# First layer's attention: the second head's q and k copied by VectorE, turned weights copied ahead of exponentials, weight roundings behind them

## What is computed

```python
def mla_mixer(c_q, c_kv, k_r, pos, q_norm, kv_norm, w_q_up, w_kv_up):
    q = (rms_norm(c_q, q_norm) @ w_q_up).reshape(B, S, MLA_HEADS, MLA_QK)
    q_nope, q_rope = q[..., :MLA_NOPE], rope(q[..., MLA_NOPE:], pos)
    kv = (rms_norm(c_kv, kv_norm) @ w_kv_up).reshape(B, S, MLA_HEADS, MLA_NOPE + MLA_V)
    k_nope, v = kv[..., :MLA_NOPE], kv[..., MLA_NOPE:]
    k_rope = jnp.broadcast_to(rope(k_r, pos)[:, :, None, :], (B, S, MLA_HEADS, MLA_ROPE))
    qf = jnp.concatenate([q_nope, q_rope], axis=-1)
    kf = jnp.concatenate([k_nope, k_rope], axis=-1)
    out = causal_block_attention(qf, kf, v, MLA_QK ** -0.5)
...
def memory_attention(q, k, v):
    s = jnp.einsum('bshd,bmhd->bhsm', q, k, preferred_element_type=jnp.float32) * (MEM_DIM ** -0.5)
    p = jax.nn.softmax(s, axis=-1)
    return jnp.einsum('bhsm,bmhd->bshd', p.astype(v.dtype), v)
```

## Time and profile before

| what | us |
|---|---|
| median of 3 runs | 1186.57 (1186.21 to 1186.69) |
| the profiled execution, device time | 1186.46 |
| its span (first to last instruction) | 1184.7 |
| TensorE busy | 1163.5 (98%) |
| ScalarE busy | 604.0 (51%) |
| VectorE busy | 540.8 (46%) |
| GpSimd busy | 459.8 (39%) |

### The profile page before, as it was taken

One profiled execution on the slowest core, in us unless ns is written; L12 is line 12 of the kernel. 1 busy time (PEld: TensorE's weight loads), 2 busy tenths in 40 slices (PEclk: granted clock), 3 DMA queues, 4 the chain that ended last, 5 costly groups with the idle time before them and its releaser, 6 DMA issues.

```text
span 1184.7 us, 16023 instructions
## 1 busy us (share of the span) xinstructions
PE 1163.5 (98%) x5967; PEld 913.9 (77%) x5967; DVE 540.8 (46%) x987; ACT 604.0 (51%) x1266; POOL 459.8 (39%) x331
## 2 busy tenths in 40 slices
PE   8999999899999999999999999999999999999998
PEld 7988866578988666668888987787666677888886
DVE  4311575645110655454466546612787860033333
ACT  7344677755352655564545654534655553243242
POOL 6534721134344222314343322445444443444461
PEclk9999999999999999999999999999999999999999
DMA  8443211113335322212331322233222113232321
GB/s 301 144 107 69 65 23 48 54 58 88 96 100 137 96 72 71 72 37 74 107 89 54 117 61 65 78 89 107 62 63 54 54 54 89 90 107 89 106 89 71
DMA packets 111573, 100.99 MB, mean 85 GB/s; under 512 B 21168, under 2 KB 98300, under 8 KB 111496
## 3 DMA queue, kind: packets, MB, share of 16 engines
q1 hardware_dynamic: 108952, 95.38, 27.6%
q0 software_dynamic: 864, 3.15, 0.7%
q10 hardware_dynamic: 1680, 1.44, 0.4%
HBM read 97.83 MB, written 2.12 MB: 84 GB/s over the span
## 4 chain that ended last, share of the span: by engine, by line
PE 91%; DVE 3%; ACT 3%; issue 2%; DMA 1%; POOL 1%; SPq 0%; DVEq 0%; ACTq 0%
PE bank L607 49%; PE bank L2054 8%; PE bank L1712 7%; PE bank L1504 6%; PE bank L912 3%; PE bank L878 3%; PE bank L896 2%; PE bank L2070 2%; PE bank L2082 2%; PE bank L2094 2%; PE bank L1296 1%; PE bank L1801 1%; DMA w_raw<-in_w_mem_kv 1%; POOL w_lo L526 1%; PE bank L717 1%
## 5 line engine op out<-in xcount | busy, mean ns | idle before, releaser
L526 POOL TENSOR_TENSOR w_lo<-w_raw,w_hi 128x1024 fp32r<-128x1024 f32 (+4 forms) x157 | 352.9, 2249 | 632.6 <-ACT w_hi L511 632.6
L511 ACT ACTIVATE w_hi<-w_raw 128x1024 fp32r<-128x1024 f32 (+6 forms) x161 | 159.2, 989 | 228.7 <-PE bank L607 200.2
L607 PE MATMUL bank<-acts_hi,w_hi 128*128 128x512 f32 (+1 forms) x576 | 224.2, 389 | 0.9 <-POOL w_lo L526 0.9
L607 PE MATMUL bank<-acts_lo,w_hi 128*128 128x512 f32 (+1 forms) x576 | 222.7, 387 | 0.0
L607 PE MATMUL bank<-acts_hi,w_lo 128*128 128x512 f32 (+1 forms) x576 | 222.6, 386 | 0.0
L607 PEld LDWEIGHTS bank<-acts_hi,w_hi 128*128 128x128 f32 x576 | 108.2, 188 | 24.4 <-POOL w_lo L526 1.5
L607 PEld LDWEIGHTS bank<-acts_lo,w_hi 128*128 128x128 f32 x576 | 108.2, 188 | 21.9
L607 PEld LDWEIGHTS bank<-acts_hi,w_lo 128*128 128x128 f32 x576 | 108.3, 188 | 21.3
L2189 DVE TENSOR_TENSOR_SCAN arena_end<-arena,junk 128x512 f32<-128x512 f32 (+3 forms) x64 | 72.8, 1138 | 58.3 <-ACT arena L2139 58.3
L607 PE MATMUL bank<-w_hi,acts_hi 128*128 128x512 f32 (+4 forms) x240 | 87.0, 362 | 0.4 <-POOL w_lo L526 0.3
L607 PE MATMUL bank<-w_hi,acts_lo 128*128 128x512 f32 (+4 forms) x240 | 86.2, 359 | 0.0
(11 more groups left out here) (307 smaller groups left out, 2153.5 us busy)
## 6 DMA issues: line engine op xcount, KB each, us to landing
w_raw<-in_w_in SPq DMA_DIRECT2D x64, 512.0 KB, 3.7
w_raw<-in_w_out SPq DMA_DIRECT2D x24, 512.0 KB, 3.6
w_raw<-in_w_in_b SPq DMA_DIRECT2D x22, 512.0 KB, 3.8
w_raw<-in_w_in_a SPq DMA_DIRECT2D x10, 512.0 KB, 4.2
w_raw<-in_w_mem_kv SPq DMA_DIRECT2D x8, 512.0 KB, 8.3
w_raw<-in_w_sb_proj SPq DMA_DIRECT2D x8, 512.0 KB, 3.4
w_raw<-in_w_ssd_proj SPq DMA_DIRECT2D x8, 512.0 KB, 3.4
arena_shared<-f_kept_rows SPq DMA_DIRECT2D x11, 256.0 KB, 4.4
```

Of the source, the lines that this page charges most:

```text
L511: nc.scalar.activation(w_at(p)[0][:, 0:size], w_raw[p % RAW][:, 0:size], ACT.Copy).then_inc(w_high.sem, 1)
L526: nc.gpsimd.tensor_tensor(lo[:, 0:size], w_raw[p % RAW][:, 0:size], hi[:, 0:size].bitcast(F32), ALU.subtract).then_inc(w_rest.sem, 1)
L607: mm = nc.tensor.matmul(bank_of(S, s, g)[0:lhs.shape[1], 0:rhs.shape[1]], lhs, rhs, start=j + kk + t == 0, stop=j == len(S.pieces) - 1 and ...
```

## The change

Three things change in steps 8 to 27 of the first layer's sweep; the number of instructions stays the same in total but for the copies' engine.

1. `collect` copies only the first head's half on ScalarE, for all products but the first two (`BY_BOTH`). The second head's half is a new VectorE instruction in `collect_second` (a multiplication by the same scale), which stands in `early` of the even steps, ahead of the maxima of the next step. It counts `qk_second`. The next product waits for both counts, and so do the first scores of a pair.
2. In the odd steps 9 to 27 the copies of turned weights run ahead of the exponentials (`copies_first`).
3. The weight rounding leaves `after` of the even step and stands in `between` of the odd step that follows, behind its exponentials.

```diff
-        def sweep_act(act, A, between, after, lag=1):
+        def sweep_act(act, A, between, after, lag=1, copies_first=()):
...
-            copies_first = (steps - 4, steps - 3, steps - 1)
+            copies_first = (*copies_first, steps - 4, steps - 3, steps - 1)
...
+        qk_second = count("qk_second")
+        BY_BOTH = 2
...
         def mla_pair(p):
+            second_in = ((qk_second.sem, 2 * p + 2 - BY_BOTH),) if p else ()
...
-                        ((qk_made.sem, 2 * p + 2), rope_in, pA_v.evac(2 * MB)))
+                        ((qk_made.sem, 2 * p + 2), rope_in, pA_v.evac(2 * MB)) + second_in)
...
                     if q:
                         pe.wait_ge(qk_made.sem, q)
+                    if q > BY_BOTH:
+                        pe.wait_ge(qk_second.sem, q - BY_BOTH)
...
+        def head_of_step(s):
+            return 2 * (s // 4 - MP) + 2 + s % 4 // 2
...
-                for e in range(2):
+                for e in range(2 if q < BY_BOTH else 1):
                     rows = slice(e * HD, (e + 1) * HD)
                     ins = nc.scalar.activation((aqT2, akT2)[q % 2][e][p % 2][rows], bank[0][rows, :], ACT.Copy,
...
                 if 4 * MP <= s < last and s % 2 == 0:
-                    q = 2 * (s // 4 - MP) + 2 + s % 4 // 2
-                    collect(q)
-                    split_ahead_act(act, S, 0, q)
+                    collect(head_of_step(s))
...
+            def between(s):
+                if 4 * MP < s <= last and s % 2:
+                    split_ahead_act(act, S, 0, head_of_step(s - 1))
...
-            sweep_act(act, attA, lambda s: None, after, lag=2)
+            sweep_act(act, attA, between, after, lag=2, copies_first=range(4 * MP + 1, last, 2))
...
+            def collect_second(q):
+
+                p, rows = q // 2, slice(HD, 2 * HD)
+                dve.wait_ge(C["product"].sem, pA_qk.done_after(0, q, 0))
+                if p >= 2:
+                    dve.wait_ge(*attA.scored(4 * (MP + p - 1)))
+                nc.vector.tensor_scalar((aqT2, akT2)[q % 2][1][p % 2][rows], bank[0][rows, :],
+                                        (QK_A ** -0.5, 1.0)[q % 2], None, ALU.mult).then_inc(qk_second.sem, 1)
...
+                if 4 * MP <= s < last and s % 2 == 0:
+                    collect_second(head_of_step(s))
```

## The result

| | before | after |
|---|---|---|
| median of 6 runs each, side by side, us | 1186.45 | 1177.3 (1176.98 to 1177.77) |
| the profiled execution, device time / span | 1186.46 / 1184.7 | 1177.3 / 1175.5 |

The ratio is 0.9924, with a 95% interval of 0.9913 to 0.9934.

What follows compares the result with a forecast made beforehand. TensorE, nearly full, was held by waits before the eight turns and the 512 scores. A limit of 8.06 less 0.5 gave 7.56, said as 7.5; from 1186.46 that made 1179.0 us, range 1177.8 to 1182.6.

Steps and rivals of the forecast that it cites:

- the VectorE-bound rival: Engines reading one bank take turns, so the q copy takes 0.60 us longer and VectorE becomes the bound; 1183.5 us, chance 0.14.
- 13.0 to 13.3: Forecast stretch in us between q products, in place of 14.71, with the first 0.4 less.
- That is a tie: From 256 maxima to second 512 scaling, VectorE needs 7.51 us and TensorE 7.61, so the q copy just fits.
- the 0.5 for it: Loss in us for the hand-over between engines, 0.1 in each pair, taken off the gain.
- VectorE's 7.51: VectorE's summed need in us from the 256 maxima to the second 512 scaling, new q copy included.
- at nothing: Cost given to the moved roundings, among other side effects, including the later GpSimd low parts.
- some 2 us later against TensorE: How much later a moved q rounding was said to end, relative to TensorE.
- the 1.40: TensorE's wait in us before the eight turns of a pair, blamed on ScalarE's late copies; all of it was to go.
- the tail ... 0.3 either way: Stretch behind the loop's end at 230.41 us, said to have the same instructions; allowed 0.3 us up or down.
- The low end of 1177.8: Fast end of the range in us: the limit of 8.06 with 0.3 from the tail and 0.3 for reading starts.
- the limit of 8.06: Most the loop of five pairs could gain in us: 69.13 less 61.07 of TensorE time without waits.
- The slower rival: GpSimd's low part for q holds the second 512 scaling, said to be clear by 1.39 us; 1191.7 us, chance 0.05.

Runs made afterwards that it cites:

- e6: The changed kernel with VectorE's copy of each second k half done twice, the extra one into scratch; 1180.06 us.
- e5: The changed kernel with VectorE's copy of each second q half done twice, the extra one into scratch; 1179.56 us.
- e3: The changed kernel with only the weight roundings put back in the even step, behind the half copy; 1180.70 us.
- e8: e3 with GpSimd made to wait, ahead of each low part, until VectorE has ended the running step's scalings; 1177.12 us.
- e12: The kernel before, with only a GpSimd wait ahead of each low part until VectorE has ended the running step's scalings; 1184.39 us.
- e2: The changed kernel with ScalarE's old order of copies, exponentials and roundings back, the second head's halves staying on VectorE; 1181.46 us.
- e7: The kernel before with one part of the change alone, copies of turned weights ahead of the exponentials in the odd steps; 1182.34 us.
- e1: The changed kernel with the second head's half copies back on ScalarE, the new order there kept; 1178.88 us.
- e9: The changed kernel with the last pair's gating product moved behind the scalings of the 256-column step; 1177.62 us.

## Why the prediction was wrong in size

**Right.** What bound the loop (the eight turns behind ScalarE's copies, the 512 scores behind the k copy), that both waits go, that TensorE is late next (busy for all of the 60.82), that the copies take 0.69, that the k copy lies inside VectorE's wait for the mask (though TensorE has only 0.06 to spare for it, e6), that a bank is read by two engines at once: the VectorE-bound rival needed turn-taking, and no row shows it. The Trainium skill (PSUM — Partial Sum Buffer, "PSUM bank collisions raise a hardware error") lets two engines read different quadrants of a bank together; the trace agrees, with 0.69 and 0.59 from the same 196.40. Pairs of 12.99 are just under the 13.0 to 13.3 that I named.

**Wrong: "That is a tie", and the 0.5 for it.** VectorE's 7.51 contained 2.96 "256 maxima, 384 scalings and the gating product". I took a stretch of the old timeline as the work in it. 0.64 of it was GpSimd holding two scalings (its low part of k the first, its copy the second), and the moved roundings take that away, so the stretch needs 7.51 - 0.64 = 6.87 against TensorE's 7.61. The copy of q must wait for the q product, so of the difference only some 0.16 can be used (e5); but that is room, not a loss. The hand-over cost nothing: 0.5 of the 1.65 by which I missed. Nor was it a tie with the hold left in: e3, which has it, takes 13.74 a pair, 0.76 more than after and not 0.1, and 0.59 of that lies where the 384 scalings and what follows them come late. I had weighed the same hold in the earlier trace rows, as a danger for the second 512 scaling, and not looked for it among the rows I was adding up.

**Wrong with it: the moved roundings "at nothing".** They cost nothing, and 3.4 us of the gain hang on them (e3), by GpSimd alone (e8). The "some 2 us later against TensorE" is wrong for q and was not asked for k: the low part of q starts 5.04 behind its q product, where it was 4.84, that of k 4.53 behind its k product, where it was 3.41. It is the 1.12 of the k part that ends the hold. I asked what a later low part would collide with, not what it would stop colliding with. With the hold gone the chain that starts at the 512 maxima starts earlier as well: e12 shows 0.53 a pair of the 1.40 that I put down to ScalarE's list going by that alone.

**Wrong: "the tail ... 0.3 either way".** It gave 0.72. ScalarE's timeline before, from the last collection on:

```profile
230.60 1.19 ACT L1357 ACTIVATE arena<-bank 64x512 f32<-64x512 f32 x2 [0.43 <-PE bank L1296]
231.82 1.06 ACT L511 ACTIVATE w_hi<-w_raw 128x1024 fp32r<-128x1024 f32 x1
...
235.55 0.69 ACT L952 ACTIVATE arena<-bank,stat 128x512 f32<-128x512 f32 x1
```

The same exponential after:

```profile
226.52 0.69 ACT L952 ACTIVATE arena<-bank,stat 128x512 f32<-128x512 f32 x1
```

Counted from the 256 scores of that pair (230.41 and 222.18), it starts at 5.14 and now at 4.34. Before, the two-half copy and a rounding of 1.06 stood ahead of what TensorE waits for. TensorE's next scores need the banks that these exponentials read; in its timeline before:

```profile
237.05 1.56 PE L878 MATMUL bank<-arena 128*128 128x384 f32 x4 [0.36 <-ACT arena L952]
```

Those scores start 6.64 behind the 256 scores before, and 6.02 after (228.20). "The same instructions" is true of the tail, but it begins with an edited collection and an edited order. The halves alone give all of it (e2: 13.63), the order alone two thirds (e7: 13.88; e1, with the moved roundings, 13.88 as well). This is the term that took the time below the range. The low end of 1177.8 left out the 0.5 and had 0.3 for the reading of starts, so the loop's 8.31 lies within it; the tail's 0.72 in place of 0.3 does not, nor does the 0.16 around the attention, for which I had no term and which stays unexplained (runs of after alone differ by up to 0.8).

**Mis-sized: the limit of 8.06.** The loop gave 8.31. The 512 scores with their mask were read as 1.93; unhindered they take 186.27 - 184.42 = 1.85. They take 1.91 to 1.94 in every run where they start behind a wait (before, e1, e6, e7, e12), so the old row had in it the wait that I was removing; the two turns ahead of them take 0.23 and not 0.20, and a pair comes to 12.99 for 13.04. 0.5 + 0.72 + 0.25, some 0.16 around the attention and the 0.06 from 7.56 to 7.5 are 1.69, by the medians 1.65.

**The slower rival** was closer than I had it. The second 512 scaling starts at 191.11 and the low part of q at 191.90: 0.79 and not 1.39, and 0.31 from the scaling's end. e3 shows the collision: VectorE loses 0.6, TensorE's eight turns 0.16 a pair, where I had priced 2.38 with a VectorE that is late by 1.39 besides.

## What to carry to other kernels

Before you add up a stretch of an old timeline as an engine's need, compare each row in it with the shortest row of the same shape: what is over that may be another engine's doing, and your edit may remove it. When an instruction moves, follow everything that it releases on other engines, and ask what those leave as well as what they meet. For a value copied out of a bank, look at who waits for the copy itself, not only at what stands behind it on the copying engine.

## What the runs showed of the hardware

VectorE's scalings in SBUF are held for a GpSimd subtraction or copy beside them: 0.42 became 0.82 to 0.84, 0.49 became 1.08, and one wait on GpSimd gave 2.1 us (e12) or 3.4 us (a ratio of 0.9951 in e3, 0.9922 in e8). A held scaling ends behind GpSimd's instruction by 0.08 with 128 columns, 0.21 with 384 (before, 188.60 against 188.39) and 0.27 with 512 (e3), where alone it takes 0.29, 0.42 and 0.49. That is 0.2 less in each case, so the prediction's slower rival, which adds the whole 0.49 behind GpSimd's end, counts 0.2 too much.

Not every VectorE instruction is held: the 512 maxima, which read banks, take 1.28 beside GpSimd's copies (after, 199.70 and 200.12) and 1.29 in e9, where GpSimd is idle. VectorE's timeline of e9:

```profile
225.34 1.29 DVE L994 TENSOR_REDUCE stat<-bank 128x1 f32<-128x512 f32 x2 [0.27 <-PE bank L885]
```

The Trainium skill (SBUF — State Buffer, "Who interferes with whom") makes this distinction between scalings and reductions; the trace agrees in both.
